# Last tile of an expert gather: VectorE takes every fourth weighted row, and TensorE's projections move up

## The reference

```python
def chunk_fn(hc):                                  # 128 tokens at a time
    ...
    expert_idx = jnp.take_along_axis(cand_idx, pos, axis=-1)
    gate = jax.nn.softmax(top_s, axis=-1)
    u = expert_u[expert_idx]
    act = jax.nn.gelu(jnp.einsum('thkd,td->thk', u, hc).astype(jnp.float32), approximate=False)
    vv = expert_v[expert_idx]
    return jnp.einsum('thk,thkd->td', (gate * act).astype(hc.dtype), vv)
...
x = x + peer_ffn(h2, ...)
return rmsnorm(x, final_g)                         # end of the first block
...
h = rms_norm(x, norm_g[l])                         # the second block begins
p = h @ w_in[l]
```

## Time and profile before

| | us |
|---|---|
| median of 3 runs | 2561.14 |
| lowest and highest | 2556.56 and 2561.56 |
| the profiled execution | 2570.31 |
| its span, first to last instruction | 2568.5 |
| TensorE busy in the span | 2246.8 |
| VectorE busy | 1697.6 |
| ScalarE busy | 869.1 |
| GpSimd busy | 870.6 |

### The profile page before, as it was taken

One profiled execution on the slowest core, in us unless ns is written; L12 is line 12 of the kernel. 1 busy time (PEld: TensorE's weight loads), 2 busy tenths in 40 slices (PEclk: granted clock), 3 DMA queues, 4 the chain that ended last, 5 costly groups with the idle time before them and its releaser, 6 DMA issues. The chain is left out here.

```text
span 2568.5 us, 33593 instructions
## 1 busy us (share of the span) xinstructions
PE 2246.8 (87%) x12054; PEld 1420.6 (55%) x12054; DVE 1697.6 (66%) x3853; ACT 869.1 (34%) x1958; POOL 870.6 (34%) x649
## 2 busy tenths in 40 slices
PE   8998999888888888777777788888889899989999
PEld 6886667753444434322223343344458788777787
DVE  7998797366666666667677767766644833646453
ACT  4222673332323232222334233423224222246441
POOL 0001213343444444433433355545521221212243
PEclk9999999999999999999999988899999999979999
DMA  4232214269999999999999999999963222332252
GB/s 152 102 111 95 79 50 173 82 250 420 409 416 410 404 417 405 418 421 419 408 417 419 413 392 404 402 406 408 419 269 135 76 75 72 107 110 89 84 194 105
DMA packets 123092, 683.04 MB, mean 266 GB/s; under 512 B 13104, under 2 KB 13488, under 8 KB 57136
## 3 DMA queue, kind: packets, MB, share of 16 engines
q0 software_dynamic: 73728, 536.90, 50.8%
q1 hardware_dynamic: 49200, 143.99, 15.8%
HBM read 659.35 MB, written 21.50 MB: 265 GB/s over the span
## 5 line engine op out<-in xcount | busy, mean ns | idle before, releaser
L1773 PE MATMUL bank<-peer_uv,peer_diag 128*128 128x512 f32 x2048 | 977.5, 622 | 246.3 <-ACT peer_diag L1400 245.9
L1650 DVE SCALAR_TENSOR_TENSOR peer_uv<-peer_uv,early_h 128x1024 f32<-128x1024 f32 x512 | 649.7, 1280 | 392.1 <-DMA peer_uv<-in_peer_uv,peer_index 391.9
L1773 PEld LDWEIGHTS bank<-peer_uv,peer_diag 128*128 128x128 f32 x2048 | 388.3, 198 | 750.6 <-issue 747.1
L1446 POOL DMA_INDIRECT peer_uv<-in_peer_uv,peer_index x512 | 541.3, 1057 | 731.4 <-PE bank L1773 647.0
L162 PE MATMUL bank<-hT_high,weight_high 128*128 128x512 f32 (+1 forms) x952 | 433.4, 455 | 13.8 <-POOL weight_low L230 8.2
L230 POOL TENSOR_TENSOR weight_low<-weight_ring,weight_high 128x1024 fp32r<-128x1024 f32 x91 | 222.3, 2443 | 651.9 <-ACT weight_high L213 651.9
L164 PE MATMUL bank<-hT_high,weight_low 128*128 128x512 f32 (+1 forms) x952 | 371.3, 390 | 0.0
L163 PE MATMUL bank<-hT_low,weight_high 128*128 128x512 f32 (+1 forms) x952 | 371.1, 390 | 0.0
L213 ACT ACTIVATE weight_high<-weight_ring 128x1024 fp32r<-128x1024 f32 x171 | 180.5, 1056 | 414.5 <-PE bank L164 414.2
L1395 ACT ACTIVATE peer_gelu<-peer_dots 128x2 f32<-128x2 f32 x256 | 52.0, 203 | 784.2 <-DVE peer_uv L1650 783.9
L162 PEld LDWEIGHTS bank<-hT_high,weight_high 128*128 128x128 f32 x952 | 182.5, 192 | 81.6 <-issue 34.6
(11 more groups left out here) (428 smaller groups left out, 2757.1 us busy)
## 6 DMA issues: line engine op xcount, KB each, us to landing
weight_ring<-in_weights SPq DMA_DIRECT2D x184, 512.0 KB, 3.3
z_store<-fill_stage SPq DMA_DIRECT2D x70, 256.0 KB, 2.4
peer_uv<-in_peer_uv,peer_index POOLq DMA_INDIRECT x512, 10.4
merge_z<-z_store SPq DMA_DIRECT2D x8, 768.0 KB, 6.4
merge_z<-z_store SPq DMA_DIRECT2D x12, 512.0 KB, 4.5
swz<-z_store SPq DMA_DIRECT2D x1, 2560.0 KB, 9.8
x<-in_x SPq DMA_DIRECT2D x4, 512.0 KB, 6.4
xqz<-z_store SPq DMA_DIRECT2D x1, 2048.0 KB, 13.7
```

The lines of the kernel that those rows point to most:

```text
L1446: pool.indirect_dma_start(uv[:, p % SLOTS], None, peer_uv, bass.IndirectOffsetOnAxis(index[:, n % 2, p % TOPK:p % TOPK + 1], 0)).then_inc( ...
L1650: nc.vector.scalar_tensor_tensor(uv[:, p % SLOTS, 0:D], uv[:, p % SLOTS, 0:D], 1.0, h2[:, t], ALU.mult, ALU.mult, accum_out=dots[:, p % TO ...
L1773: mm = nc.tensor.matmul(bank[2 * t + c][:], diag[:, p % SLOTS], uv[:, p % SLOTS, D + c * 512:D + (c + 1) * 512], start=(h == 0 and p % TOP ...
```

## The change

In the last tile VectorE takes every fourth pick, `p % 4 == 3`, the second one of each odd group. For such a pick ScalarE writes no diagonal and TensorE has no matmul. VectorE multiplies the row with its weight and adds it to `x[:, 3]` itself (`add_pick`, 32 in all, right behind the choosing steps of that group). `vector_added` counts these adds; GpSimd waits for it before it fills the slot again, and `finish(3)` waits for all 32. The waits on `diag_ready` are counted anew (`diags_up_to`). From `Z_FROM` on TensorE takes 4 steps of `early_z` in an odd group and 2 in an even one (`z_steps`), in place of 2 in each, and `z_group` follows. The computed result is the same sum in another order.

```diff
--- before.py
+++ after.py
@@ -1158,9 +1158,36 @@
 Z_OFFSET = 183264
 
 
+LAST_TILE = (TT - 1) * PH * TOPK
+
+
+def on_vector(p):
+
+    return p >= LAST_TILE and p % 4 == 3
+
+
+def diags_up_to(p):
+
+    return p - max(p - LAST_TILE, 0) // 4
+
+
+def adds_up_to(g):
+
+    return max(GROUP * (g + 1) - LAST_TILE, 0) // 4
+
+
+def z_steps(g):
+
+    return 0 if g < Z_FROM else 2 + 2 * (g % 2)
+
+
 def z_group(n):
 
-    return Z_FROM + (DT * (n + 1) - 1) // 2
+    g, done = Z_FROM - 1, 0
+    while done < DT * (n + 1):
+        g += 1
+        done += z_steps(g)
+    return g
 
 
 def mem_group(k):
@@ -1223,6 +1250,7 @@
         key_squared, key_mean, key_root, key_rstd_ready, key_normed, key_turned = (st.sem(f"key_{n}") for n in (
             "squared", "mean", "root", "rstd", "normed", "turned"))
         kv_kept, kv_stored = st.sem("kv_kept"), st.sem("kv_stored")
+        vector_added = st.sem("vector_added")
         z_kept, last_act, last_dve, last_high = (st.sem(n) for n in ("z_kept", "last_act", "last_dve", "last_high"))
         iota = const.whole("iota").rearrange("p (a b) -> p a b", a=TOPK)
         u0, m0, r0 = first_unit("query"), first_unit("mem"), first_unit("rwkv")
@@ -1397,6 +1425,8 @@
                     if g >= RINGS:
                         act.wait_ge(summed, g - RINGS + 1)
                     for p in picks(g):
+                        if on_vector(p):
+                            continue
                         nc.scalar.activation(diag[:, p % SLOTS], ident, ACT.Copy,
                                              scale=weight[:, p % TOPK:p % TOPK + 1]).then_inc(diag_ready, 1)
                     if scores < QUERIES and score_group(scores) < g:
@@ -1416,9 +1446,10 @@
                 for n in range(zs, Z_UNITS - 1):
                     next(norming[TT - 1], None)
                     keep_z(n)
-                for _ in range(4 - (Z_UNITS - 1 - zs)):
-                    next(norming[TT - 1])
-                keep_z(Z_UNITS - 1)
+                if zs < Z_UNITS:
+                    for _ in range(4 - (Z_UNITS - 1 - zs)):
+                        next(norming[TT - 1])
+                    keep_z(Z_UNITS - 1)
                 for _ in norming[TT - 1]:
                     pass
 
@@ -1442,6 +1473,8 @@
                         pool.wait_ge(index_ready, n + 1)
                     if g >= RINGS:
                         pool.wait_ge(summed, g - RINGS + 1)
+                        if adds_up_to(g - RINGS):
+                            pool.wait_ge(vector_added, adds_up_to(g - RINGS))
                     for p in picks(g):
                         pool.indirect_dma_start(uv[:, p % SLOTS], None, peer_uv,
                                                 bass.IndirectOffsetOnAxis(index[:, n % 2, p % TOPK:p % TOPK + 1], 0)
@@ -1550,13 +1583,23 @@
                     if q == 0:
                         dve.wait_ge(recip_ready, n + 1)
                     if g >= GROUPS:
-                        dve.wait_ge(diag_ready, TOPK * n + (GROUP * (q + 1) - TOPK))
+                        dve.wait_ge(diag_ready, diags_up_to(TOPK * n + (GROUP * (q + 1) - TOPK)))
                     nc.vector.scalar_tensor_tensor(weight[:, at], gelu[:, at], r[:, b:b + 1], e[:, b, at], ALU.mult,
                                                    ALU.mult).then_inc(weight_ready, 1)
 
+                def add_pick(g, p):
+
+                    dve.wait_ge(weight_ready, g + 1)
+                    if adds_up_to(g) > 1:
+                        dve.wait_ge(vector_added, adds_up_to(g) - 1)
+                    nc.vector.scalar_tensor_tensor(x[:, TT - 1], uv[:, p % SLOTS, D:2 * D], weight[:, p % TOPK:p % TOPK + 1],
+                                                   x[:, TT - 1], ALU.mult, ALU.add).then_inc(vector_added, 1)
+
                 def finish(t):
 
                     dve.wait_ge(summed, groups_up_to(t))
+                    if t == TT - 1:
+                        dve.wait_ge(vector_added, PH * TOPK // 4)
                     for c in range(2):
                         part = x[:, t, c * 512:(c + 1) * 512]
                         nc.vector.tensor_tensor(part, bank[2 * t + c][:], part, ALU.add).then_inc(added, 1)
@@ -1660,6 +1703,9 @@
                     weigh(g, n, q)
                     if q >= 2:
                         next(ahead, None)
+                    for p in picks(g):
+                        if on_vector(p):
+                            add_pick(g, p)
                     if q == GROUPS - 1:
                         for _ in ahead:
                             pass
@@ -1768,11 +1814,13 @@
                         pe.wait_ge(first_kept, QUERIES)
                     pe.wait_ge(arrived[g % RINGS], 16 * GROUP * (g // RINGS + 1))
                     for p in picks(g):
-                        pe.wait_ge(diag_ready, p + 1)
+                        if on_vector(p):
+                            continue
+                        pe.wait_ge(diag_ready, diags_up_to(p) + 1)
                         for c in range(2):
                             mm = nc.tensor.matmul(bank[2 * t + c][:], diag[:, p % SLOTS],
                                                   uv[:, p % SLOTS, D + c * 512:D + (c + 1) * 512],
-                                                  start=(h == 0 and p % TOPK == 0), stop=(h == PH - 1 and p % TOPK == TOPK - 1))
+                                                  start=(h == 0 and p % TOPK == 0), stop=(h == PH - 1 and p % TOPK == TOPK - 1 - (t == TT - 1)))
                     mm.then_inc(summed, 1)
                     for _ in range(side_steps(g)):
                         next(side, None)
@@ -1781,8 +1829,7 @@
                     for i, at in enumerate(FINISH_AT):
                         if g == at + FINISH_PE:
                             turn(i)
-                    if g >= Z_FROM:
-                        next(early, None)
+                    for _ in range(z_steps(g)):
                         next(early, None)
                 for _ in early:
                     pass
```

## The result

The changed kernel is slower. Over 20 runs each its median was 2566.11 us against 2557.48 us for the kernel before; the ratio is 1.0027 with a 95% interval of 1.0015 to 1.0039, or about 7 us (the two medians lie 8.6 us apart, which the interval covers). Run a second time it gave 1.0027 again (1.0012 to 1.0041). The forecast was 1.6 us less, with 0.57 on no change to be told.

A forecast was written before the change was run, and what follows sets the result against it. The prediction took transfers plus some stalls to bound the last tile and the norm's chain its end; loads +3.7, adds +0.8, stalls -3.5 and end -2.6 gave -1.6 us, so 2559.5 us, range 2553 to 2567.

The forecast's parts named there:

- The bound: Last tile: limited by DMA transfers plus 8.9 us of stalls; after the last gather: limited by the norm's chain, not projections.
- The loads: Last tile's gather: three weight loads moved into it share the DMA engines at 1.25 us each, +3.7 us.
- The adds: Last tile: VectorE's 32 adds mostly fit into its waits for rows; +0.8 us, between 0 and +4.
- What the stalls give back: Last tile: lighter TensorE shortens what follows a held VectorE dot where the late group is odd; -3.5 us.
- The end: After the last gather: shorter last sum and earlier root, partly offset by slower transposes; -2.6 us, ends -3.8 and -0.7.
- VectorE becomes the bound: Groups 192 to 212: the adds leave VectorE too little room to absorb delays; +7 us, 2568 us, chance 0.14.
- GpSimd is held by the adds: Last tile: each add holds a GpSimd indirect issue, up to 41 us, +10 after absorption; 2571 us, chance 0.04.
- HAM oscillation — how this bites in real kernels: Last tile: TensorE waiting between short bursts could run at its low clock throughout; +5 us, no separate chance.

The follow-up runs named there:

- adds_on_top: Kernel before, with both VectorE and TensorE adding every fourth row of the last tile, two projection steps per group: ratio 1.0008, last tile 345.0 us.

## Why the prediction was wrong

**The bound** was read rightly, as far as the runs show: the last tile is bound by transfers less some stalls, and the end by the norm's chain.

**The sum** was +3.7 + 0.8 - 3.5 - 2.6 = -1.6 us. There is a path of kernels from the one to the other, each with one part more. From 345.5 us, the quicker steps with their loads bring 350.0 (+4.5), the left-out rows 352.6 (+2.6), the adds 356.7 (+4.1). Another path goes over the left-out rows, 351.1 on the mean of two (+5.6), the adds, 351.8 (+0.7), and the steps with their loads (+4.9). So, term by term:

- The loads: +3.7 forecast. With the quicker steps they are 4.5 and 4.9 us; taken out alone they are 6.1 by the profiles of the changed kernel and 5 to 6 by its ratios, and 7.9 by one pair of profiles (350.0 and 342.1) but 3.6 by the ratios (0.9984 and 0.9970) with the picks on TensorE. Right in kind and, within what the runs can tell, in size.
- The adds: +0.8 forecast. With two steps they cost nothing that shows, -0.5 us (`adds_on_top`) and +0.7, with ratios that allow 2 us more. With the quicker steps they measure +4.1 us, and 4.9 us is what separates the changed kernel with idle matmuls and late loads from the kernels that leave TensorE its picks. So this term was probably too small by 3 to 4 us; why it grows with the quicker steps stays open.
- **What the stalls give back: 3.5 us forecast, with 0 as the lower end. This is the step that failed.** The lighter TensorE gives nothing back but costs 2.6 to 5.6 us, a miss of 6 to 9 us, the largest of the sum. I had written that a late group's aftermath is shortened where it is odd. What the runs show in its place is a TensorE that is more often at 1.2 GHz: the clock from 1660 to 1840 us fell from 0.94 and 0.96 in the two profiles to 0.91 and 0.89 with the picks gone, and rose to 0.95 and 0.96 with idle matmuls in their place. Between two levels, 1 and one half, 0.89 is 22% of the time at the lower one, 0.94 is 12%. The rate went with it (411 and 412, then 401 and 404, then 407 and 412 GB/s), and so did the slow sums. The price fits, where eight records after an idle gap took 5.37 and 6.46 us and not 3.60. I had used just this for group 254 at the end and for the transposes, but not for the 31 odd groups ahead of it.
- The end: -2.6 forecast, -3.7 measured. Half of the last sum saved its full 1.7 us, since group 255 ran warm (1.96 us); the way from the mean to the transposes, with the root, became 2.2 us shorter; the transposes lost 0.9. That is 3.0 us, the difference of the first two profiles (20.94 and 17.90 us); the second profile of the kernel before had an end of 22.6 us.

**The rivals.** "VectorE becomes the bound" gave +7 us and 0.14, and the number came true, but not where it said. The loss is not in the first third: groups 192 to 210 took 106 us in the changed kernel and 105 before. VectorE had 141 us of work in 180, near the 144 that I had worked out, and 32 adds on the unchanged TensorE cost nothing that shows. That the number matched is luck, though the adds' part with the quicker steps may be a smaller form of this rival, later in the tile. "GpSimd is held by the adds" is borne out only a little: the mean indirect issue of the last tile took 1.17 to 1.20 us in the kernels with 32 adds and 1.09 to 1.14 in those without, some 5 to 9 us in all, and `adds_on_top` still had 415 GB/s. The mechanism of the largest miss was the one of the Trainium skill's "TensorE: Matmul & The Clock Gate", section "HAM oscillation — how this bites in real kernels": short bursts between waits for data bring the clock down again and again. By that rule the trace agrees in kind: from 1672 to 1852 us the clock was 0.90 against 0.95, though TensorE was busy 147 of these 180 us and far from cold all the way. I had priced it at +5 us and then put it away inside another rival, with the argument that TensorE soon comes back to 3.60 us a group. It does, but each slow sum frees its slots late, and the changed kernel had 18 and 20 of them in place of 9 and 10. How much of that comes through the clock and how much through the later diagonals was not measured apart. As a rival of its own, with a fair chance, it would have moved the whole forecast.

**The check that was at hand.** The earlier trace rows shows the clock at 0.91 where the rate is 405, 0.95 at 410 and 1.00 at 420 and 421. I read the low clock as a companion of TensorE's overload. It went with its idle gaps, and the change made these longer (78.1 us of waits for diagonals in place of 44.3). The pattern is no law: the changed kernel had 0.87 at 409 GB/s and 0.92 at 421.

## What to carry to other kernels

In a gather that keeps the DMA engines full, expect a weight load that is moved into it to cost its bytes at the full rate: here three loads cost 3.6 to 7.9 us, with 3.7 by their bytes. A load that nobody needs soon belongs behind the gather, even when the work that frees its place is moved up. And work taken from a TensorE that is already waiting can lengthen the loop: see what the granted clock does beside its idle gaps, and if it falls there, try giving TensorE more to do, not less. A cost measured beside one load need not hold beside another: the adds cost nothing that shows with two steps, and about 4 us by the profiles with the quicker ones. A change that gains only at a stage's end is best cut down to that end: here one row on VectorE and one swapped pair on ScalarE did better than 32 rows.

## What the runs showed that I had not expected

Two idle matmuls of 128 by 512 in every odd group, which compute nothing that is used, shortened the last tile by 4.1 us on the mean of two profiles (351.1 to 347.0), and brought the granted clock from 0.91 and 0.89 to 0.95 and 0.96. That was with the rows left out and two steps; in the changed kernel the times show no such gain. More useful work does the same: with up to 5.5 us of it in an odd group by my estimate, and its loads kept out, TensorE ran at 0.99 and the gather at 419 GB/s, the nearest of all to the undisturbed 421. The transposes at the end took 1.97 us after 8.19 us of idle time, against 1.09 after 2.04.
